# Attention and retention encoder on one core: new opening, new borders between the layers, gate unit in three steps

## What is computed

```python
for layer in range(DEPTH):                       # DEPTH = 2
    h = rms_norm(x, norm_g[layer])
    z = h @ w_in[layer]
    qa, ka, va, ga, qr, kr, vr, gr, gm = split_columns(z)
    # A: 8 query heads, 2 key/value heads of 64; norms and axial rotations of q and k, softmax
    ya = (silu(ga) * attention(qa, ka, va)) @ w_branch_attn[layer]
    # B: 4 heads of 128, rotations, a forward and a backward scan with decays, group norm
    yb = (silu(gr) * retention(qr, kr, vr)) @ w_branch_ret[layer]
    x = x + (sigmoid(gm[0]) * ya + sigmoid(gm[1]) * yb) @ w_out[layer]
return rms_norm(x, final_norm_g)
```

## Time and profile before

| engine | busy, us | share | instructions |
|---|---|---|---|
| PE (matmul) | 1812.3 | 94% | 10784 |
| PE (weight load) | 1590.6 | 82% | 10784 |
| DVE | 1061.7 | 55% | 2246 |
| ACT | 668.2 | 35% | 1564 |
| POOL | 836.7 | 43% | 652 |

### The profile page before, as it was taken

One profiled execution on the slowest core, in us unless ns is written; L12 is line 12 of the kernel. 1 busy time (PEld: TensorE's weight loads), 2 busy tenths in 40 slices (PEclk: granted clock), 3 DMA queues, 4 the chain that ended last, 5 costly groups with the idle time before them and its releaser, 6 DMA issues.

```text
span 1929.7 us, 32806 instructions
## 1 busy us (share of the span) xinstructions
PE 1812.3 (94%) x10784; PEld 1590.6 (82%) x10784; DVE 1061.7 (55%) x2246; ACT 668.2 (35%) x1564; POOL 836.7 (43%) x652
## 2 busy tenths in 40 slices
PE   3899989999999999999878998999999999999995
PEld 3788978899999888888667887789999988888874
DVE  6979678635554210107977987794444541110478
ACT  4368438622212100003433872683222210000133
POOL 3348337623422323335823773485223422323383
PEclk9999999999999999999989999999999999999998
DMA  7100000101111111124130001001011111112132
GB/s 248 33 12 13 27 23 23 45 23 44 35 30 34 44 55 44 44 65 164 34 124 23 23 1 49 9 15 45 24 43 43 44 33 44 44 54 65 50 136 88
DMA packets 129593, 96.40 MB, mean 50 GB/s; under 512 B 15664, under 2 KB 114224, under 8 KB 129456
## 3 DMA queue, kind: packets, MB, share of 16 engines
q1 hardware_dynamic: 125920, 84.56, 14.1%
q10 hardware_dynamic: 3536, 10.17, 1.5%
HBM read 82.13 MB, written 12.58 MB: 49 GB/s over the span
## 4 chain that ended last, share of the span: by engine, by line
PE 69%; DVE 16%; issue 6%; DMA 3%; ACT 2%; POOL 2%; DVEq 1%; SPq 1%; ACTq 0%; POOLq 0%
PE ps L566 17%; PE ps L568 17%; PE ps L567 17%; PE ps L701 5%; PE ps L690 4%; DVE xh L1711 3%; PE ps L714 2%; PE ps L716 2%; DMA xh<-xs 2%; PE ps L807 2%; DVE pT_lo L1477 1%; PE ps L791 1%; DVE zqk L1388 1%; DVE rtb L1396 1%; DVE hT_lo L1698 1%
## 5 line engine op out<-in xcount | busy, mean ns | idle before, releaser
L566 PE MATMUL ps<-w_hi,hT_hi 128*128 128x256 f32 (+1 forms) x1280 | 390.3, 305 | 13.9 <-DVE hT_lo L1343 9.3
L568 PE MATMUL ps<-w_hi,hT_lo 128*128 128x256 f32 (+1 forms) x1280 | 376.5, 294 | 0.0
L567 PE MATMUL ps<-w_lo,hT_hi 128*128 128x256 f32 (+1 forms) x1280 | 376.3, 294 | 0.0
L383 POOL TENSOR_SCALAR w_hi<-raw 128x1024 fp32r<-128x1024 f32 x100 | 108.4, 1084 | 398.5 <-PE ps L568 368.4
L566 PEld LDWEIGHTS ps<-w_hi,hT_hi 128*128 128x128 f32 x1280 | 245.0, 191 | 17.4 <-issue 12.5
L566 PE MATMUL ps<-hT_hi,w_hi 128*128 128x512 f32 x640 | 254.6, 398 | 0.0
L567 PE MATMUL ps<-hT_lo,w_hi 128*128 128x512 f32 x640 | 251.1, 392 | 0.0
L568 PE MATMUL ps<-hT_hi,w_lo 128*128 128x512 f32 x640 | 250.8, 392 | 0.0
L567 PEld LDWEIGHTS ps<-w_lo,hT_hi 128*128 128x128 f32 x1280 | 245.2, 192 | 0.3
L568 PEld LDWEIGHTS ps<-w_hi,hT_lo 128*128 128x128 f32 x1280 | 244.6, 191 | 0.0
L389 POOL TENSOR_TENSOR w_lo<-raw,w_hi 128x1024 fp32r<-128x1024 f32 x84 | 207.5, 2470 | 6.0
(11 more groups left out here) (175 smaller groups left out, 3543.0 us busy)
## 6 DMA issues: line engine op xcount, KB each, us to landing
raw<-w_in SPq DMA_DIRECT2D x168, 256.0 KB, 3.2
xs<-xh SPq DMA_DIRECT2D x2, 4096.0 KB, 17.6
xh<-xs SPq DMA_DIRECT2D x8, 1024.0 KB, 13.9
xh<-x ACTq DMA_DIRECT2D x4, 1024.0 KB, 10.1
raw<-w_a SPq DMA_DIRECT2D x16, 256.0 KB, 2.9
raw<-w_r SPq DMA_DIRECT2D x16, 256.0 KB, 3.2
w<-w_o SPq DMA_DIRECT2D x4, 1024.0 KB, 11.6
ctA<-rope_a SPq DMA_DIRECT2D x8, 256.0 KB, 2.9
```

Source lines behind the costliest of these rows:

```text
L383: nc.gpsimd.tensor_scalar(place(pos)[0], raw[:, slot], 1.0, 1.0, ALU.mult, ALU.mult).then_inc(w_rounded, 1)
L566: nc.tensor.matmul(outp, ah, bh, start=(start and i == 0), stop=False)
L567: nc.tensor.matmul(outp, ah, bl, start=False, stop=False)
L568: last = nc.tensor.matmul(outp, al, bh, start=False, stop=(stop and i == len(pairs) - 1))
```

## The change

It does six things.

- Opening. SP and ACT issue the loads at once, without waiting for the constants, and x comes in single tiles at first. The first three weight units are loaded beside it, rounded by ACT (`first_hi`, L1043) and subtracted by DVE (`first_lo`, L1418). Squares are of whole rows (`square_row`, L1038), and those of tiles 2 to 7 stand behind ACT's outputs of tiles 0, 1 and 2. The mean squares are of rows 0, 1, 2 and 3, and 4 to 7. The decays move from ahead of the first norm into the projection, at tiles 2, 4 and 6.
- The loop over the layers is written out on all engines, and the drains and waits at its border are gone. Inner loops over heads are written out on SP.
- The output products 3, 4 and 5 change places, so that rows 0 to 3 of x are complete after the fifth product and not after the sixth.
- Beside them, all lower halves of the weights (`right_lo`, 14 instructions a layer) move from POOL to DVE, and the left sums of products 5 and 6 from DVE to POOL.
- At the border DVE norms tiles 0 and 1 of the next layer before it adds up product 5, and PE turns them between the row blocks of its last product, which goes block by block (`last_product`). At the end of the program DVE norms rows 0 to 3 before it adds up the last two products, and takes two mean squares of two rows for the rest; ACT stores tiles 5 and 7, SP the others.
- The second gate unit of an attention projection is rounded after the rotation of tile 3 and subtracted in halves after those of tiles 4 and 5.

The core of the diff:

```diff
-LEFT = (((1, 0, 1),), ((0, 0, 1), (0, 1, 1)), ((0, 0, 1), (1, 0, -1)), ((1, 0, 1), (1, 1, 1)),
-        ((1, 0, 1), (0, 1, 1)), ((0, 1, 1),), ((1, 1, 1), (0, 1, -1)))
+LEFT = (((1, 0, 1),), ((0, 0, 1), (0, 1, 1)), ((0, 0, 1), (1, 0, -1)), ((1, 0, 1), (0, 1, 1)),
+        ((0, 1, 1),), ((1, 0, 1), (1, 1, 1)), ((1, 1, 1), (0, 1, -1)))
...
-ORDER_SUM = (2, 1, 3, 4, 6)
+ORDER_SUM = (2, 1, 3, 5, 6)
+A_SLOT = (0, 1, 2, 3, 0, 1, 3)
...
+            xt = x.rearrange("(t p) d -> p t d", p=P)
+            sp.dma_start(xh[:, 0, 0:512], xt[:, 0, 0:512]).then_inc(x_in[0], 16)
+            for slot in range(2):
+                for a in (0, K // 2)[:1 + slot]:
+                    sp.dma_start(*cols_of(raw[:, slot], 0, C_QA + slot * P, a)).then_inc(raw_in[slot], 16)
+            for s, c0 in ((0, C_KA), (1, C_VA)):
+                sp.dma_start(raw3[:, :, s * HD:(s + 1) * HD],
+                             w_in[bass.ds(0, DM), bass.ds(c0, HD)].rearrange("(k p) c -> p k c", p=P)).then_inc(raw3_in, 16)
+            for i in range(1, 4):
+                sp.dma_start(xh[:, i], xt[:, i]).then_inc(x_in[i], 16)
...
                         if t == 3:
                             pool.wait_ge(b_proj, L * (KVH * T) + j * T + T)
-                            fill(0, 0, L * PER[0] + j * 3 + 2, n0 + j * N_B + 4)
+                            fill_hi(0, 0, L * PER[0] + j * 3 + 2)
+                        if t in (4, 5):
+                            fill_lo_part(0, 0, n0 + j * N_B + 4, t - 4)
...
+                def left_sum(p):
+                    pool.wait_ge(d_mg, L * (2 * K) + 2 * K + 1)
+                    pool.wait_ge(o_sum, L * N_SUM + 2 * ORDER_SUM.index(p))
+                    pool.wait_ge(o_done, L * (4 * N_P) + 4 * N_P + 4 * ({5: 1, 6: 3}[p] + 1))
+                    (r, kr, _), (q, kq, sign) = LEFT[p]
                     for h in range(2):
-                        pool.wait_ge(o_bhi, L * (2 * N_P) + 2 * p + h + 1)
-                        hi, lo = right_slot(p, h)
-                        nc.gpsimd.tensor_tensor(lo, right_src(p, h), hi.bitcast(F32), ALU.subtract).then_inc(o_blo, 1)
+                        nc.gpsimd.tensor_tensor(left_total(p, h), left(r, kr, h), left(q, kq, h),
+                                                ALU.add if sign > 0 else ALU.subtract).then_inc(o_sum, 1)
                 right_sum(0, 2)
-                right_lo(0)
-                right_lo(1)
                 right_sum(2, 4)
-                right_lo(2)
-                right_lo(3)
-                right_sum(4, 6)
-                right_lo(4)
-                right_sum(5, 8)
-                right_lo(5)
+                right_sum(3, 6)
+                right_sum(4, 8)
+                left_sum(5)
                 right_sum(6, 10)
-                right_lo(6)
+                left_sum(6)
...
+                def last_product(p):
+                    base = L * N_POST + N_POST
+                    pe.wait_ge(o_alo, L * (2 * N_P) + 2 * ORDER_A.index(p) + 2)
+                    pe.wait_ge(o_blo, L * (2 * N_P) + 2 * N_P + 2 * p + 2)
+                    for i in range(4):
+                        pe.wait_ge(o_post, base + POSTS[p - 2] + len(INTO[p - 2]) * (i + 1))
+                        o = ps[:, O_BANK[p] + i, :]
+                        o = o.rearrange("p (a b) -> p a b", b=256 if p in IN_W else 512)
+                        for k in range(4):
+                            bh, bl = right_tile(p, k)
+                            ah, al = left_tile(p, k, i)
+                            nc.tensor.matmul(o, ah, bh, start=(k == 0), stop=False)
+                            nc.tensor.matmul(o, ah, bl, start=False, stop=False)
+                            mm = nc.tensor.matmul(o, al, bh, start=False, stop=(k == 3))
+                        mm.then_inc(o_done, 1)
+                        if L + 1 < DEPTH and i >= 1 and i <= 2:
+                            pe.wait_ge(o_post, base + POSTS[p - 1] + len(INTO[p - 1]) * (2 * i))
+                            turn_x(i - 1, L + 1)
+                for p in range(N_P - 1):
                     o_product(p)
-                pe.drain().then_inc(phase_end, 1)
+                last_product(N_P - 1)
...
+            def square_row(t):
+                act.wait_ge(x_in[t if t < 4 else 2 + t // 2], 16 if t else 32)
+                if t:
+                    act.wait_ge(a_sq, t)
+                nc.scalar.activation(junk2[:], xtile(t), ACT.Square, accum_out=ss4[:, t:t + 1]).then_inc(a_sq, 1)
+            def first_hi(i):
+                act.wait_ge(raw3_in if i == 2 else raw_in[i], 32)
+                nc.scalar.copy(w_hi[:, :, i * P:(i + 1) * P], raw3[:] if i == 2 else raw[:, i]).then_inc(w_rounded, 1)
+            square_row(0)
+            act.wait_ge(idf_in, 16)
+            nc.scalar.copy(idr[:], idf[:]).then_inc(pro_act, 1)
+            first_hi(0)
+            first_hi(1)
...
                     if j == 0:
+                        act.wait_ge(o_done, L * (4 * N_P) + 4 * (N_P - 2))
                         hi_x(0)
+                        if L == 0:
+                            first_hi(2)
+                            square_row(1)
                     for t in range(T):
                         if j == 0 and t + 1 < T:
                             hi_x(t + 1)
                         if j == 0 and t == 0:
+                            act.wait_ge(o_done, L * (4 * N_P) + 4 * N_P)
+                        if j == 0 and t == 0 and L:
                             act.wait_ge(o_post, L * N_POST + N_POST)
                             for i in range(4):
-                                square(4 + i, 0, L * N_SQ + 12 + i, sqj)
+                                square(4 + i, 0, SQ0(L) + 12 + i, sqj)
                         outputs(t)
+                        if j == 0 and L == 0:
+                            if t < 3:
+                                square_row(2 + 2 * t)
+                                square_row(3 + 2 * t)
+                            if t == 3:
+                                act.wait_ge(pro_dve, 2)
+                                nc.scalar.activation(lgw[:, 2], lgw[:, 1], ACT.Exp).then_inc(pro_act, 1)
+                            if t == 5:
+                                act.wait_ge(pro_dve, 22)
+                                nc.scalar.activation(dec[:, :, 0:6], dec[:, :, 0:6], ACT.Exp).then_inc(pro_act, 1)
...
+            mean_square(0, 1, 1, 0)
+            dve.wait_ge(gain_in, 16)
+            norm_x(0, 0)
+            first_lo(0)
+            first_lo(1)
...
+                    if j == 0 and L == 0:
                         lo_x(0)
-                        norm_x(L, 2)
+                        first_lo(2)
+                        mean_square(1, 2, 2, 12)
+                        norm_x(0, 1)
                     for t in range(T):
                         if j == 0 and t + 1 < T:
-                            lo_x(t + 1)
+                            if L == 0 or t > 0:
+                                lo_x(t + 1)
+                            if L == 0 and t < 2:
+                                if t == 0:
+                                    mean_square(2, 4, 4, 24)
+                                norm_x(0, t + 2)
                             if t == 1:
-                                mean_square(L, 1)
-                            if t + 3 < T:
+                                mean_square(4, 8, SQ0(L + 1) if L == 0 else SQ0(L) + N_SQ, 36 if L == 0 else NW_0 + L * NW_L + 12)
+                            if t + 3 < T and (L or t):
                                 norm_x(L, t + 3)
+                        if j == 0 and L == 0:
+                            if t == 2:
+                                decays_start()
+                            if t == 4:
+                                decays_ratio()
+                            if t == 6:
+                                decays_end()
...
+                def right_lo(p):
+                    if p == 0:
+                        dve.wait_ge(o_blo, L * (2 * N_P) + 2 * N_P)
+                    for h in range(2):
+                        dve.wait_ge(o_bhi, L * (2 * N_P) + 2 * p + h + 1)
+                        hi, lo = right_slot(p, h)
+                        V.tensor_tensor(lo, right_src(p, h), hi.bitcast(F32), ALU.subtract).then_inc(o_blo, 1)
                 left_sum(2)
                 left_lo(0)
                 left_lo(2)
+                right_lo(0)
                 merge(K - 1)
                 left_sum(1)
                 left_lo(1)
+                right_lo(1)
+                left_sum(3)
                 add_up(0)
-                left_sum(3)
+                right_lo(2)
                 left_lo(3)
                 add_up(1)
-                left_sum(4)
+                right_lo(3)
                 left_lo(4)
                 add_up(2)
+                right_lo(4)
+                right_lo(5)
                 left_lo(5)
                 add_up(3)
-                left_sum(6)
                 left_lo(6)
+                right_lo(6)
```

(33 more changed lines are left out.)

289 lines of the change are left out of this document (150 added, 139 removed).

## The result

The changed kernel is 0.6% slower, which is clear of the noise. Its four runs give 1945.02 to 1948.61, median 1945.76; the kernel before, timed beside it, 1934.57. The ratio is 1.0062, 95% interval 1.0045 to 1.0079, so +8.7 to +15.3 us, +12.0 in the middle. The forecast was 1948.4, +14.3 on the profiled execution, whose span went from 1929.7 to 1944.2: +14.5. The profiled execution of before lay 3 us under its median, that of the changed kernel (1945.98) at its own, which is why the medians differ by less.

The account below looks back on a forecast made before the run. TensorE was taken as the bound, its matmuls filling 1812.3 of 1929.7 us. Opening 10.9, split −1.2, border 0.2 and end 4.4 gave +14.3 on 1931.5, 1945.8; with 2.6 for the median 1948.4, range 1926 to 1957.

Parts of the forecast that it names:

- First product at 19.6: Opening: PE's first product starts at 19.6 us, 13 us earlier than before, since a single x tile is normed at once.
- Third group at 33.1: Opening: PE's transposes of tile 2 start at 33.1 us, after 7.2 idle, waiting for squares behind ACT's outputs of tile 0.
- Fifth at 53.3: Opening: PE's transposes of tile 4 start at 53.3 us instead of 49.18, rows 6 and 7 being squared late.
- Lower half of tile 4 at 62.1, +6.9: Opening, on DVE: the lower half of tile 4's transpose starts at 62.1 us instead of 55.22, 6.9 later.
- Decays +4.0: Opening: the decays' small DVE steps, formerly free under the loads, now cost 4.0 us in DVE's full stretch at tile 4.
- Split −1.2: Attention projections: filling the second gate unit in three POOL steps between rotations saves 0.3 us each, 1.2 in all.
- Additions 4 at +51.3 us from the end of the first ones: Output products: product 4's additions on DVE end 51.3 us after the first additions, at 955.4 instead of 952.5.
- Border +0.2: Between the layers: the new order gives nothing, 985.7 against 985.5 before, +0.2 us; bounds −10.9 to +9.6.
- the free port: Rival, output products: POOL's ten remaining instructions block nothing on DVE, total −7.5, giving 1926.6 us; chance 0.15.
- End +4.4: End of the program: DVE chain +1.5 us and later additions +2.9, together +4.4; bounds −6.3 to +13.8.
- the kept lead: Rival, opening: the stretch before tile 4 is not the chain, −9.2 us instead of +10.9, giving 1928.3; chance 0.10.
- Slow first weights: Rival, opening: weights loaded beside x come slowly, the first product starts 6 us later, giving 1954.4 us; chance 0.15.

Follow-up runs that it names:

- Experiment 1: Changed kernel with ACT's row squares of tiles 2 to 5 right behind tile 1's, and those of 6 and 7 ahead of the first outputs: 1934.68 us, ratio 1.0008.
- experiment 7: Changed kernel with the second gate unit filled in one go behind the rotation of tile 3, as in the kernel before: 1945.50 us, ratio 1.0065.
- experiment 4: Changed kernel with POOL's sums of right blocks covering only 8 columns of each block row, values partly left out: 1925.59 us, ratio 0.9962.
- Experiment 3: Changed kernel with the right blocks' lower halves back on POOL and the left sums of products 5 and 6 back on DVE: 1940.13 us, ratio 1.0036.
- Experiment 5: Changed kernel with POOL starting the second layer's first weight units only after DVE's norms of tiles 0 and 1: 1939.20 us, ratio 1.0036.

## Why the prediction was right

The forecast named the sign, the size and most of the places. That the total agrees to 0.2 us (14.5 against 14.3) is luck. By the table, its misses are +1.5 up to scores 1, +1.0 up to scores 3 and +0.8 at the end, against −0.1, −1.1, −0.9 and −1.0 in the other stretches. By its steps:

- *First product at 19.6*: 20.76. *Third group at 33.1*: 33.87. *Fifth at 53.3*: 53.09. *Lower half of tile 4 at 62.1, +6.9*: 61.51, +6.3. Experiment 1 shows that ACT's order makes it.
- *Decays +4.0*: the step is right, its size too small. Their removal brought the first scores 6.5 us forward. I priced the steps alone; the 5.25 us for which PE stood idle behind them also lowered its clock, 2.1 us more. So the opening gave +12.1 with nothing for the split, where I had 10.9 and −0.3.
- *Split −1.2*: in sum wrong, 0 within what can be told (experiment 7). The rows bear the working out on DVE (1.1 and 0.8 lost by the halves, where I had 1.1 and 0.6, against 2.1). What failed is the step from there to PE: its waits for the queries did not shrink with DVE's loss, 20.6 us against 18.3 with the unit whole. The Trainium skill (SBUF — State Buffer, SBUF: two separate sides) says that the port pair of the two engines is locked for a whole instruction; by that alone I had worked out 0 for this term and left it aside. The trace agrees with it here, and in experiment 4, where a POOL sum of 128x16 takes 1.1 us beside DVE and 0.2 alone.
- *Additions 4 at +51.3 us from the end of the first ones*: 50.56, +2.3 on before where I had 2.9. Experiment 3 shows that it is the move of the lower halves (3.1 us, less 0.8 that the new order gives), experiment 4 that it is POOL beside them. The items are less right than their sum: no pair took 6.9, two neighbours took 4.55 each where I had 6.9 and 2.3, and DVE waited 1.04 for ACT, which I had not.
- *Border +0.2*: additions 4 to the end of the first product 31.6 us, I had 30.3. POOL met more of the roots and norms than before (12.7 us for mean square and norms, I had taken 10.65). PE's idle stretch inside product 6 was 15.2, not 13. Experiment 5 takes 7.7 us off. A slip in the sums: the lower bound of this step should be −10.5, not −10.9 (944.7 is 10.7 before 955.4), which would put the free port at 1927.0; nothing hangs on it.
- *End +4.4*: +5.2. I had 31.4 us behind additions 4 and it is 32.9: the mean square after the last additions waits 2.44 for ACT's squares, which I had left out of the chain.
- *Not foreseen*: 1.1 and 1.0 us less in the stretches between second scores and first additions of each layer, in which the loops were written out and the lower halves of the first two right blocks moved to DVE. Experiment 3 moves these back and has the same (618.7 and 619.0 us), so it is not they. No run takes the loops apart; the cause stays open. The fourth head group was 1.2 shorter where I had 0.3; it lies between 166.0 and 168.0 in the runs.

The free port fell with the pairs at 4.55 in the changed kernel and with experiment 4, the kept lead with the two 7 us stretches. Slow first weights did not come: ACT rounds the first two units at 9.81 and the third at 13.12 without a wait for them. It had stood 3.95 us for the load of the identity just before, though, which may have hidden one.

## What to carry to other kernels

An early start is worth what the queue order of every engine behind it lets through. Write down, for each early piece, which instruction of a slower engine's queue it must pass, and put preparations for later tiles ahead of the outputs of the present one. Where two engines shut each other out for whole instructions, moving work from one to the other or cutting it in pieces need not gain anything: here the move cost 3 us a layer and the splitting gave nothing. Better is to give the second engine its work beside instructions that aren't blocked, here those with an operand in PSUM. That took 4 us off the stretch in layer 1, until PE and the producers of the right blocks became the chain. Count the wait for every producer in a final chain, small squares too, and reduce the number of roots there. And follow a block to the wait of the engine that bounds the kernel before you price it: DVE lost a little less with the split unit, and PE waited no less.
